# Inverting 64x64 blocks on TensorE: full-array product with zero blocks, the first four levels as a loop, key scores and values after it

## The reference

```python
def step(S, inp):
    r_t, w_t, k_t, v_t, kk_t, b_t = inp
    sa = jnp.einsum('bhvk,bhk->bhv', S, -kk_t)
    S = S * w_t[:, :, None, :] + sa[..., None] * b_t[:, :, None, :] + v_t[..., None] * k_t[:, :, None, :]
    return S, jnp.einsum('bhvk,bhk->bhv', S, r_t)
```

## Time and profile before

| | us |
|---|---|
| three runs | 2096.29, 2100.78, 2100.33 (median 2100.33) |
| the profiled execution | 2097.18 |
| its span in the trace | 2095.4 |
| TensorE busy in it | 2023.3 (97%) |
| VectorE, ScalarE, GpSimd busy | 1266.3, 897.4, 147.4 |

### The profile page before, as it was taken

How to read it: one execution, slowest core, us unless ns; L and a number is a source line. 1 busy time by engine, 2 the same in 40 slices (tenths; PEclk the granted TensorE clock), 3 DMA queues, 4 the chain that set the end, 5 groups by cost and what they waited for, 6 DMA issues and landing times.

```text
span 2095.4 us, 32769 instructions
## 1 busy us (share of the span) xinstructions
PE 2023.3 (97%) x12954; PEld 1628.9 (78%) x12954; DVE 1266.3 (60%) x1545; ACT 897.4 (43%) x1235; POOL 147.4 (7%) x180
## 2 busy tenths in 40 slices
PE   7987999999999999999999999999999999999999
PEld 6677778878668878978878678877856888897887
DVE  7764665557665545665667655567865554566553
ACT  4443244434544434444545444434423444434442
POOL 2231110010010001000002011000000000000000
PEclk9999999999999999999999999999999999999999
DMA  8301165546256564555555257553312655555554
GB/s 298 129 23 45 48 210 183 187 156 207 81 162 206 182 203 161 171 195 187 166 185 191 74 168 224 188 191 125 114 54 92 200 189 182 170 171 181 184 174 143
DMA packets 92522, 335.32 MB, mean 160 GB/s; under 512 B 11150, under 2 KB 11284, under 8 KB 92095
## 3 DMA queue, kind: packets, MB, share of 16 engines
q1 hardware_dynamic: 85536, 311.62, 44.9%
q0 software_dynamic: 6880, 22.16, 3.7%
HBM read 332.69 MB, written 1.05 MB: 159 GB/s over the span
## 4 chain that ended last, share of the span: by engine, by line
PE 88%; DVE 6%; issue 2%; POOL 2%; ACT 1%; DMA 0%; SPq 0%; DVEq 0%; ACTq 0%; POOLq 0%
PE acc L326 40%; PE acc L403 20%; PE acc L379 10%; PE acc L853 2%; DVE w_lo L1460 2%; PE aux L774 1%; PE aux L984 1%; PE aux L977 1%; PE aux L809 1%; POOL rstd L2222 1%; PE acc L579 1%; POOL stat L2225 1%; PE aux L841 1%; PE aux L423 1%; DVE token_scratch L1536 1%
## 5 line engine op out<-in xcount | busy, mean ns | idle before, releaser
L1460 DVE TENSOR_TENSOR w_lo<-w_raw,w_hi 128x1024 fp32r<-128x1024 f32 x588 | 716.2, 1224 | 588.5 <-ACT w_hi L1102 584.1
L1102 ACT ACTIVATE w_hi<-w_raw 128x1024 fp32r<-128x1024 f32 x588 | 620.3, 1059 | 802.6 <-PE acc L326 463.8
L326 PE MATMUL acc<-w_hi,operand_hi 128*128 128x512 f32 x1344 | 535.2, 398 | 26.6 <-DVE operand_lo L1615 12.2
L326 PE MATMUL acc<-w_hi,operand_lo 128*128 128x512 f32 x1344 | 526.0, 391 | 0.0
L326 PE MATMUL acc<-w_lo,operand_hi 128*128 128x512 f32 x1344 | 525.2, 391 | 0.0
L326 PEld LDWEIGHTS acc<-w_hi,operand_hi 128*128 128x128 f32 x1344 | 253.8, 189 | 88.3 <-DVE operand_lo L1481 15.0
L326 PEld LDWEIGHTS acc<-w_hi,operand_lo 128*128 128x128 f32 x1344 | 253.4, 189 | 54.2
L326 PEld LDWEIGHTS acc<-w_lo,operand_hi 128*128 128x128 f32 x1344 | 254.0, 189 | 50.5 <-issue 0.5
L403 PE MATMUL acc<-w_hi,hidden_hi 128*128 128x512 f32 x528 | 210.2, 398 | 0.0
L403 PE MATMUL acc<-w_hi,hidden_lo 128*128 128x512 f32 x528 | 208.5, 395 | 0.0
L403 PE MATMUL acc<-w_lo,hidden_hi 128*128 128x512 f32 x528 | 208.5, 395 | 0.0
(11 more groups left out here) (429 smaller groups left out, 2115.1 us busy)
## 6 DMA issues: line engine op xcount, KB each, us to landing
w_raw<-in_weights SPq DMA_DIRECT2D x588, 512.0 KB, 3.4
ln_gain<-in_gains POOLq DMA_DIRECT2D x7, 512.0 KB, 5.3
bias_at<-in_rpb POOLq DMA_DIRECT2D x12, 256.0 KB, 5.3
ln_gain<-in_ln_g POOLq DMA_DIRECT2D x4, 512.0 KB, 3.9
ln_bias<-in_ln_b POOLq DMA_DIRECT2D x4, 512.0 KB, 5.3
vec_rw<-in_vec POOLq DMA_DIRECT2D x3, 512.0 KB, 7.2
l_rw<-in_lora SPq DMA_DIRECT2D x1, 1152.0 KB, 10.6
iclr_rw<-in_xT SPq DMA_DIRECT2D x2, 512.0 KB, 4.6
```

Source lines behind the costliest of these rows:

```text
L326: mm = pe.matmul(acc[:, 2 * pair + t, :], (ah, al)[x][:, kt, t * P:(t + 1) * P], W[w][:, s, kk * 512:(kk + 1) * 512], start=(kt == 0 and ( ...
L1102: act.activation(whi[:, s, :], raw[:, s, :], ACT.Copy).then_inc(w_hi[s], 1)
L1460: dve.tensor_tensor(wlo[:, s, :], raw[:, s, :], whi[:, s, :].bitcast(F32), ALU.subtract).then_inc(w_lo[s], 1)
```

## The change

- NM becomes two tensors of 128 partitions by 128 columns for each pair of heads: chunk s stands in rows of half s and columns of the other half, and the other two blocks are zero, set once by GpSimd. A product is then 8 calls on the whole array in place of 16 on quarters. NM0 takes the memory of the layer norm's gain and bias, so load_ln(0) moves behind the last product. ScalarE copies N in halves (8 copies for 4).
- TensorE runs the first four levels (16 steps) as a loop of four rounds of four steps, each: wait for t_copied(g) and e_copied(g - 2), product(g + 2), extension(g). The loop's start waits for rb_copied and for both inverses (inv_set).
- The last level is unrolled, and keys(0) to keys(3) stand behind its four extensions; keys_by_values stands by itself, behind W.
- VectorE: set_keys behind masked products 16 to 19, the other passes earlier. ScalarE: rhs behind the copies of W.

The diff, cut to its core:

```diff
+    [NM0] = scope(("n_first", [P, 2, KT, P]))
...
-        NM, INV, INVT = rwkv("n_rw", [P, TT, 2, KT, CH]), rwkv("inv_rw", [P, TT, 2, KT, CH]), rwkv("invt_rw", [P, TT, 2, KT, CH])
+        [NM1] = scope(("n_second", [P, 2, KT, P]))
+        SPARE, INV, INVT = rwkv("n_room", [P, 2, KT, P]), rwkv("inv_rw", [P, TT, 2, KT, CH]), rwkv("invt_rw", [P, TT, 2, KT, CH])
...
-    GN = tok
+    GN, NM = tok, (NM0, NM1)
...
-            pe.wait_ge(m["n_copied"], due(m["n_copied"], 2))
+            pe.wait_ge(m["e_copied"], 2)
...
-            def product(g, with_values=None):
-                u, b = g % UNITS, g % 2
+            def product(u):
                 for kt in range(KT):
-                    for s in range(2):
-                        of = half_of(s)
-                        mm = pe.matmul(ps(b)[half_of(1 - s), kt * CH:(kt + 1) * CH], NM[of, u // 2, u % 2, kt, :], INVT[of, u // 2, u % 2, kt, :],
-                                       start=(kt == 0), stop=(kt == KT - 1), skip_group_check=True)
-                    if with_values is not None:
-                        keys_by_values(with_values, kt)
+                    mm = pe.matmul(ps(u % 2)[:, kt * CH:(kt + 1) * CH], NM[u // 2][:, u % 2, kt, :], INVT[:, u // 2, u % 2, kt, :],
+                                   start=(kt == 0), stop=(kt == KT - 1))
                 mm.then_inc(m["t_ready"], 1)
-            def extension(g):
-                n, u = g // UNITS, g % UNITS
+            def step_ready(copies):
+                pe.wait_ge(m["t_copied"], due(m["t_copied"]))
+                pe.wait_ge(m["e_copied"], due(m["e_copied"], copies))
+            def extension(u, final=False):
                 t, e = u // 2, u % 2
-                pe.wait_ge(m["t_copied"], due(m["t_copied"]))
-                if g == 0:
-                    pe.wait_ge(m["rb_copied"], due(m["rb_copied"], 2))
-                elif g >= 2:
-                    pe.wait_ge(m["e_copied"], due(m["e_copied"], 2 if g - 2 < last * UNITS else 1))
-                b = 2 + u if n == last else 2 + 2 * (g % 2)
+                b = 2 + u if final else 2 + 2 * (u % 2)
...
             def keys(k):
-                if k == 0:
-                    pe.wait_ge(m["inv_set"], due(m["inv_set"], 2))
-                else:
+                if k:
                     pe.wait_ge(m["akrk_copied"], due(m["akrk_copied"]))
                 by_both_rows(6, k // 2, k % 2, KTT)
...
-            def keys_by_values(u, kt):
-                t, e = u // 2, u % 2
-                if u == 0 and kt == 0:
+            def keys_by_values(t):
+                if t == 0:
                     pe.wait_ge(m["akrk_copied"], due(m["akrk_copied"]))
                     pe.wait_ge(m["v_centred"], due(m["v_centred"]))
-                elif u == 2 and kt == 0:
+                else:
                     pe.wait_ge(m["rhs_copied"], due(m["rhs_copied"]))
-                for s in range(2):
-                    of = half_of(s)
-                    mm = pe.matmul(ps(6 + e)[of, kt * CH:(kt + 1) * CH], AKRK[of, t, e, kt, 0, :], V[of, t, head(e, kt)],
-                                   start=(kt == 0), stop=(kt == KT - 1), skip_group_check=True)
-                if e and kt == KT - 1:
-                    mm.then_inc(m["av_ready"], 1)
-            between = {0: lambda: keys(0), 2: lambda: keys(1), 4: lambda: keys(2), 6: lambda: keys(3)}
-            values_in = {14: 0, 15: 1, 18: 2, 19: 3}
-            pe.wait_ge(m["n_copied"], due(m["n_copied"], 2))
+                for e in range(2):
+                    mm = by_chunks(2 * t + e, 6 + e, by_key(0), tokens(V))
+                mm.then_inc(m["av_ready"], 1)
+            pe.wait_ge(m["e_copied"], 2 * TT)
             product(0)
             product(1)
-            for g in range(UNITS * len(STEPS)):
-                extension(g)
-                if g + 2 < UNITS * len(STEPS):
-                    product(g + 2, values_in.get(g + 2))
-                if g in between:
-                    between[g]()
+            pe.wait_ge(m["rb_copied"], due(m["rb_copied"], 2))
+            pe.wait_ge(m["inv_set"], due(m["inv_set"], 2))
+            with due.loop(last, {m["t_copied"]: UNITS, m["e_copied"]: 2 * UNITS}):
+                for u in range(UNITS):
+                    step_ready(2)
+                    product((u + 2) % UNITS)
+                    extension(u)
+            for u in range(UNITS):
+                step_ready(2 if u < 2 else 1)
+                if u < 2:
+                    product(u + 2)
+                extension(u, final=True)
+                keys(u)
             for u in range(UNITS):
                 if u >= 2:
                     pe.wait_ge(m["e_copied"], due(m["e_copied"]))
                 by_chunks(u, u, matrix(INVT), tokens(KK)).then_inc(m["w_ready"], 1)
+            for t in range(TT):
+                keys_by_values(t)
...
+                if t == 0:
+                    act.wait_ge(m["n_zeroed"], due(m["n_zeroed"], TT))
                 for e in range(2):
-                    act.activation(NM[:, t, e], heads_of(e), ACT.Copy).then_inc(m["n_copied"], 1)
+                    for s in range(2):
+                        last = act.activation(NM[t][half_of(s), e, :, half_of(1 - s)], heads_of(e)[half_of(s)], ACT.Copy)
+                    last.then_inc(m["e_copied"], 1)
...
-                if g in (14, 18):
-                    rhs((g - 14) // 4)
...
+            for t in range(TT):
+                rhs(t)
...
-            between = {2: lambda: set_keys(0), 3: lambda: bonus(0), 4: lambda: set_keys(1), 5: lambda: bonus(1), 6: lambda: set_keys(2),
-                       7: lambda: means(0), 8: lambda: set_keys(3), 9: lambda: means(1), 10: lambda: centred(0), 11: lambda: centred(1),
-                       12: lambda: biased(0), 13: lambda: biased(1)}
-            between.update({14 + k: lambda k=k: ahead(q + 20 + k, 1) for k in range(4)})
+            between = {2: lambda: bonus(0), 3: lambda: bonus(1), 4: lambda: means(0), 5: lambda: means(1), 6: lambda: centred(0), 7: lambda: centred(1),
+                       8: lambda: biased(0), 9: lambda: biased(1), 16: lambda: set_keys(0), 17: lambda: set_keys(1), 18: lambda: set_keys(2), 19: lambda: set_keys(3)}
+            between.update({11 + k: lambda k=k: ahead(q + 20 + k, 1) for k in range(4)})
...
-        load_ln(0)
...
+            pool.memset(NM0[:], 0.0).then_inc(m["n_zeroed"], 1)
...
+                    pool.memset(NM1[:], 0.0).then_inc(m["n_zeroed"], 1)
...
+            pool.wait_ge(m["t_ready"], due(m["t_ready"], UNITS * len(STEPS)))
+            load_ln(0)
```

More of the change, by code:

```diff
@@ L220, in program @@
         "exp_ready", "k_and_bonus", "scaled_ready",
-        "cum_zeroed", "masks_in", "masks_built", "t_reset",
+        "cum_zeroed", "masks_in", "masks_built", "t_reset", "n_zeroed",
         "rows_turned", "rows_copied_a", "rows_copied_v",
-        "n_ready", "n_copied", "rb_ready", "rb_copied", "akrk_ready", "akrk_copied", "inv_set",
+        "n_ready", "rb_ready", "rb_copied", "akrk_ready", "akrk_copied", "inv_set",
         "t_ready", "t_copied", "e_ready", "e_copied",
@@ L599, in extension @@
                                        start=(kt == 0), stop=(kt == KT - 1), skip_group_check=True)
-                    if n < last:
+                    if not final:
                         for s in range(2):
```

## The result

| | us |
|---|---|
| the kernel before, four runs on one chip | 2099.36 median (2096.29 to 2100.78) |
| the changed kernel, four runs on the same chip | 2159.56 median (2157.81 to 2161.88) |
| ratio | 1.0295, 95% interval 1.0281 to 1.0309 |
| span of the profiled execution, before and after | 2095.4 and 2157.3 |

The change costs 60 us, where 17 were forecast; the measured time lies outside the range. The page of the changed kernel: the busy times answer to the earlier trace rows, and the line of the granted clock, in 40 slices of 54 us, shows what is new.

A forecast was written before the change was run, and what follows sets the result against it. Instruction fetching for TensorE was taken to bound the inversion. U's end moving from 201.5 to 218.2 gave +16.7 us (2.7 at the start, loop about even, 14 in the tail); added to 2098.6, 2115.3 us, range 2106 to 2131.

The forecast's parts named there:

- the body stays in TensorE's memory: First four levels: the loop's 640 instructions and waits stay in memory, so no fetch binds its 2.91 us steps.
- a gap at each fourth step: Sign in the loop that, like packets each 4 to 5 us, would show instructions being fetched anew; that rival had 0.17.
- step 2: Start of the inversion: products 0 and 1 take 1.71 us each, the loop starts at 139.2; 2.7 us lost.
- step 3: The loop: 16 steps of 2.91 us, 46.6 us in all, ending at 185.8; about breaks even.
- The clock falls: Rival, in the loop: short matmuls and idling halve TensorE's clock; 37 us more, 2152 us; chance 0.05.
- Stretches as broken as the tail kept 1.00: Argument against a falling clock: earlier stretches as broken as the tail, idling 2.25 of 4.15 us, held full clock.
- Half the columns is far from 3: Argument against a falling clock: products stream 64 columns, unlike line 486's matmuls with 3, where the clock halved.
- factor of 0.87: Multiplier in the loop's half-clock price: 16 x 2.66 x 0.87 = 37 us more.
- The weight load does not hide: Denies a rival: a product costs only its stream, 0.88 us; within 0.2% (chance 0.06) or faster, 2094 us (0.08).
- Fetching anew: Rival, in the loop: each of three jumps back waits 3.5 to 3.9 us; +11, 2126 us; chance 0.17.
- It does not do what it says: Rival, in the loop: fetching was not the bound, so no gain; +20 us; no separate chance, counted with the forecast.
- steps 4 and 5: Tail: last level as a serial chain, 18.4 us to 204.2; then W, values, rhs and U, 14.0 to 218.2.

The follow-up runs named there:

- loops written out: The whole-array kernel with VectorE's inverse moved early, and the rearranged version, each with its loop unrolled: ratios 1.0101 (looped 1.0089) and 1.0003 (looped 0.9965).
- filled run: The changed kernel with three dummy 128x512 matmul calls in TensorE's pause before the loop: 2114.51 us, ratio 1.0097 to the kernel before.
- rearranged version: The changed kernel with quarters for all but a product's first call, VectorE's inverse earlier and the tail's serial chain broken up: 2086.49 us, ratio 0.9965.
- new product in the old order: The kernel before, unrolled and in its old order, with only the whole-array product and its zeroed storage new: ratio 1.0148, 31 us slower.

## Why the prediction was wrong

**The bound** was read right, as the loops written out show. The forecast that the body stays in TensorE's memory was right too: 640 instructions went round with no packet but in the first round. The gap of up to 0.17 us at each jump back in the filled run comes without a packet, so the prediction's sign "a gap at each fourth step" would have pointed at the wrong rival. The Trainium skill's rule in "Runtime: NRT & Kernel Launch", section "Instruction fetch mechanics", that a jump out of a two-page window stalls for a fetch, does not hold for this loop; its figure of 2,048 instructions for TensorE is not contradicted.

**The prices of the sum** were right at full clock. The filled run gives them: product to extension 1.92 us (136.00 to 137.92, forecast 1.71 + 0.10), a step 3.02, with the jumps 3.06 (2.91), from the loop's end to U's end 33.2 (32.4). In sum 20 us where 16.7 were forecast; the 0.15 a step too few is 2.4 of the rest. TensorE's pause before the loop stood in step 2 as times (the products end at 136.6, the loop starts at 139.2), 2.6 us, and was 2.64.

**What failed** is the full clock that step 3 takes for granted: 16 x 2.91 = 46.6 us, where the loop took 16 x 5.52 = 88. The rival "The clock falls", with 0.05, had it. It was ruled out on two grounds, both wrong in use. "Stretches as broken as the tail kept 1.00": those rows were of quarters, which stream most of the time, and they were held against idling in the tail, while the pause that mattered is step 2's, right between products that stream little. Nor did it hold in the tail: with pauses of 1.8 to 2.0 us the clock fell there in six of the ten traces of the changed kernel and the runs. "Half the columns is far from 3": the loop indeed keeps a clock that it has, as the filled run shows; but once lost it was not won back (0.50 through all 16 steps), and the prediction never asked how the clock would return. Its price, 37 us more for half clock throughout, was near: 16 x (5.52 - 3.02) = 40, and 60 - 20 = 40. That is in part luck: its factor of 0.87 comes from no row (by these steps it is 2.50 of 2.66, 0.94), and it left out the tail, 38.8 us in the changed kernel for 33.2. So the mechanism and about its price stood in the text; its chance was wrong, and the pause of step 2 was not seen as its start.

**The other rivals.** The weight load does not hide: the filled run's first 32 matmuls take 3.71 us, 0.116 each at full clock, where 0.107 was taken. Fetching anew did not happen. "It does not do what it says" is ruled out: written out, the rearranged version loses 8 us. Above all, the prediction's strongest part, that the change loses even if all goes well (20 us), stands: the new product trades waits for instructions against weight loads of twice the width, and the tail's chain costs what steps 4 and 5 said. The rearranged version takes back both.

## What to carry to other kernels

A change that makes matmuls short beside their weight loads must be priced at both clocks, and the question is not only whether it lowers the clock but whether it could raise it again: look for the pause just ahead of it and move the work that causes it, here four lines on another engine. Run it several times: a kernel on such an edge shows itself in one execution of four. A loop pays where the page's "issue" pieces come one per packet and the steps stay shorter than a packet takes to fetch; count instructions per us before and after. A stretch that waits on fetching hides other work for free, and that work shows up again when it is moved out.

## What the runs showed of the hardware

- What TensorE's clock is depends on what went before. The same loop of sixteen steps ran at 1.00 throughout (filled pause) or at 0.50 throughout (changed kernel), with 2.64 us ahead of it filled or not.
- TensorE at 10.00 us busy of 10.00 can stay at half clock: 90 us long, from 140 to 230, and 37 us in the new product in the old order.
- Doubling what streams beside each weight load brought the clock back before the loop's second product, and cost nothing that can be told at full clock (a product 1.93 us in both).
- A pause of 3.20 us between products and extensions in quarters left the clock at 1.00; 2.64 us between whole-array products did not, and neither did 1.82 us in quarters (rearranged, written out) or 2.0 us (last level of the run with the product in quarters). How much lies in the pause's length, in its moment and in what stood around it is open. That two of eight executions with the pause removed were as slow as the changed kernel says that chance has a part.
- Quarters brought the clock back where they ran without a pause (140.8 to 144.2, 192.8 to 196.2 us). Between pauses it stayed low longer: in the last level of the whole-array loop written out it was at half from 191 to 208 us, where extensions and key scores alternate with waits of 2 us, and came back in W.
- Alternating between whole array and quarters at each call costs 0.63 us for six matmuls. The clock fell some 10 us into it, with no pause ahead.
